# An input projection's four groups formed as seven quarter products instead of eight, in a hybrid stick-breaking and mLSTM block on Trainium2

## What is computed

```python
u = _rmsnorm(h, pre_norm_w[i])
proj = u @ w_in[i]                      # 2048 x 1024 by 1024 x 4616
sb_q, sb_k, sb_v, sb_z, ml_q, ml_k, ml_v, ml_o, ml_z, ml_i, ml_f = _split_cols(proj)
y_sb = _stick_breaking_attention(...)   # 8 heads of 64, causal
qk = silu(_causal_conv(concat([ml_q, ml_k]), ml_conv_w[i], ml_conv_b[i]))   # 4 taps over tokens
y_ml = _mlstm_chunkwise(...)            # 4 heads of 128
y = concat([y_sb, y_ml]) @ w_out[i]     # after norms and gates
h = h + _rmsnorm(y, post_norm_w[i])
h = h + sigmoid(h @ ple_w_gate[i] + ple_b_gate[i]) * (p[i] @ ple_w_up[i])
```

## Time and profile before

| what | us |
|---|---|
| runs | 1811.83, 1808.72, 1812.38; median 1811.83 |
| span of the profiled execution | 1808.6 |
| its own time beside the span | not recorded; the runs' median is 3.2 above the span, their least 0.1 |
| first stage, tiles / groups / gates on TensorE | 8.2 to 116 / 116 to 472 / 472 to 487 |
| TensorE busy | 1761.9, 97% |
| VectorE, ScalarE, GpSimd busy | 1119.1, 991.3, 680.6 |

### The profile page before, as it was taken

The page is one execution under the profiler, slowest core; times in us unless marked ns, Lnnn a source line. Parts: engine busy times, 40 slices in busy tenths (PEclk is TensorE's granted clock), DMA queues, the critical chain, the costliest instruction groups (busy, mean ns, idle before and its releaser), DMA issues. The chain is left out here.

```text
span 1808.6 us, 28177 instructions
## 1 busy us (share of the span) xinstructions
PE 1761.9 (97%) x8972; PEld 1437.3 (79%) x8972; DVE 1119.1 (62%) x1776; ACT 991.3 (55%) x2041; POOL 680.6 (38%) x942
## 2 busy tenths in 40 slices
PE   7999999999899999999999999998999999999998
PEld 6888888878577887888878887886788888788887
DVE  5431214555479898979797979894666666533333
ACT  5431213322277787878787878784677776411111
POOL 1100000000147777777777777772234444200000
PEclk9999999999999999999999999999999999999999
DMA  6677766121394647454656453735555454422220
GB/s 199 163 192 215 232 186 186 52 87 47 126 282 131 172 144 212 135 175 135 174 171 185 135 176 127 249 118 190 169 193 159 162 189 139 162 77 79 81 82 40
DMA packets 193733, 277.05 MB, mean 153 GB/s; under 512 B 66684, under 2 KB 128380, under 8 KB 184408
## 3 DMA queue, kind: packets, MB, share of 16 engines
q1 hardware_dynamic: 190952, 265.19, 47.8%
q0 software_dynamic: 2672, 10.52, 1.7%
HBM read 187.41 MB, written 88.26 MB: 152 GB/s over the span
## 5 line engine op out<-in xcount | busy, mean ns | idle before, releaser
L975 PE MATMUL b_late<-w_split,spare 128*128 128x512 f32 x1416 | 411.4, 415 | 2.5 <-ACT b_p_out L1057 2.3
L756 POOL TENSOR_TENSOR b_a_lo<-b_aT,b_a_hi 128x512 fp32r<-128x512 f32 (+2 forms) x312 | 354.8, 1137 | 25.0
L1138 DVE TENSOR_TENSOR_SCAN b_buf<-b_y,b_buf 128x511 f32<-128x511 f32 (+2 forms) x320 | 357.9, 1118 | 9.1
L529 PE MATMUL a_po<-uT_hi,w_split 128*128 128x512 f32 x1024 | 318.6, 392 | 2.3 <-DVE w_split L397 2.3
L975 PEld LDWEIGHTS b_late<-w_split,spare 128*128 128x128 f32 x1416 | 243.4, 190 | 40.5 <-issue 4.6
L752 POOL CAST b_a_hi<-b_aT 128x512 fp32r<-128x512 f32 (+1 forms) x320 | 182.1, 569 | 179.1 <-PE b_o L949 147.6
L1148 DVE SCALAR_TENSOR_TENSOR b_buf<-b_buf,b_y 128x512 f32<-128x512 f32 (+2 forms) x320 | 187.9, 587 | 70.0 <-PE b_y L935 69.0
L529 PEld LDWEIGHTS a_po<-uT_hi,w_split 128*128 128x128 f32 x1024 | 193.0, 188 | 46.4 <-DVE w_split L397 2.7
L1034 ACT ACTIVATE b_aT<-b_turned 128x512 f32<-128x512 f32 (+1 forms) x320 | 170.3, 532 | 67.6 <-POOL b_a_lo L756 60.1
L529 PE MATMUL a_po<-uT_lo,w_split 128*128 128x512 f32 x512 | 201.6, 394 | 0.0
L1043 ACT ACTIVATE b_buf<-b_y 128x512 f32<-128x512 f32 (+2 forms) x320 | 171.3, 535 | 50.1 <-PE b_y L929 47.7
(11 more groups left out here) (244 smaller groups left out, 3359.6 us busy)
## 6 DMA issues: line engine op xcount, KB each, us to landing
spare<-u_pair SPq DMA_DIRECT2D x62, 1024.0 KB, 5.4
proj_n<-b_p_out SPq DMA_DIRECT2D x59, 256.0 KB, 5.7
c_gates<-proj_n SPq DMA_DIRECT2D x16, 768.0 KB, 4.5
w_raw<-in_w_in POOLq DMA_DIRECT2D x5, 2048.0 KB, 10.1
x_in<-in_x SPq DMA_DIRECT2D x16, 512.0 KB, 3.9
qk_hi<-stage_hi SPq DMA_DIRECT2D x32, 256.0 KB, 2.6
qk_lo<-stage_lo SPq DMA_DIRECT2D x32, 256.0 KB, 2.9
u_pair<-uT_hi SPq DMA_DIRECT2D x16, 512.0 KB, 3.7
```

Source lines behind the costliest of these rows:

```text
L529: mm = pe.matmul(po[t][:], w[:, k, m * P:(m + 1) * P], u[:, k, t * GROUP:(t + 1) * GROUP], start=(k == 0 and n == 0), stop=(k == KT - 1 an ...
L756: nc.gpsimd.tensor_tensor(lo[:, cols], raw, hi[:, cols].bitcast(F32), ALU.subtract).then_inc(lo_done, 1)
L975: mm = pe.matmul(late[:], u_in[f % US][:, u_part, k, :], w[:, k, :], start=(i == 0), stop=(i == PASSES - 1))
L1138: nc.vector.tensor_tensor_scan(down, y[u % YS][:, 1:keys][:, ::-1], down, b[:, keys - 1:keys], ALU.add, ALU.subtract).then_inc(log_done, 1)
```

## The change

The 16 tiles are done in two blocks of eight. After the tiles of a block come its gate columns, and then its eight quads. A quad is 256 output columns by 1024 tokens of one of the groups 4, 5, 0, 1 (in this order, two quads a group; the first four of a block are convolved). In a quad, weights and activations are each cut in halves of depth and of columns or tokens, and the product of 2 by 2 quarters is formed as seven quarter products instead of eight (a Strassen-Winograd scheme). Each is 4 depth tiles by 3 parts, 12 matmuls of 128x128 by 128x512, whose moving side is four runs of 128 tokens.

- The four sums of activation quarters (t1 to t4) are formed once a block, during its tiles 4 to 7, t1 and t2 by VectorE, t3 and t4 by GpSimd, then split into hi and lo (`token_sums`, `high_t`, `low_t`).
- The four sums of weight quarters (s1 to s4) are formed by GpSimd in each quad, and GpSimd, not VectorE, makes the lo part of all seven weight operands (`low`). GpSimd's queue loads a quad's weights, 1 MB in rows of 1 KB, after the sixth lo part of the quad before (`load_pair`).
- The banks X, Y and Z take the products. ScalarE copies the first product out (`copy_p1`), VectorE forms the four outputs from it and the banks. The convolution's first tap and bias are a ScalarE activation that reads PSUM; VectorE adds the other three, also out of PSUM, and the few tokens across tile ends on their own (`halo_taps`).
- The loops over groups are written out. The late group's weights go to a place of their own and are split in the last four quads.
- In the second stage the first late tile's 24 matmuls are all at step 0 and before its score, the constants are waited for after it, and the clearing of semaphores follows the constants and the mLSTM's. The load of that tile's activations is now the last thing that the first stage issues, and that stage waits for all its stores to land.

The core of the diff, with TensorE's, ScalarE's, VectorE's and GpSimd's new order:

```diff
+PRODUCTS = (("a11", "b11", "x", True), ("s2", "t2", "y", True), ("a12", "b21", "x", False), ("s3", "t3", "y", False),
+            ("s1", "t1", "z", True), ("a22", "t4", "y", False), ("s4", "b22", "z", False))
@@ tensor
+            def product(q, s):
+                pe.wait_ge(op_lo_done, SLOTS * q + s + 1)
...
+                if s == 2:
+                    pe.wait_ge(p1_done, q + 1)
+                if s == 3:
+                    pe.wait_ge(u2_done, q + 1)
+                if s == 5:
+                    pe.wait_ge(u3_done, q + 1)
+                if s == 6:
+                    pe.wait_ge(c22_done, q + 1)
...
+                for k in range(HALF):
+                    for m, (w_part, u_part) in enumerate(PARTS):
+                        mm = pe.matmul(out, w_ops[:, s, w_part, k, :], u[home][:, :, u_part, k, :],
-            with pe.Fori(1, GROUPS) as g:
-                group(g)
+            turn(0)
+            for b in range(BLOCKS):
...
+                values(TILES * b + TILES - 1)
+                for h in range(2):
+                    gates(2 * b + h)
+                for q in range(PER * b, PER * (b + 1)):
+                    for s in range(SLOTS):
+                        if q == PER - 1 and s == SLOTS - 1:
+                            turn(TILES)
+                        product(q, s)
@@ scalar
+            def high(t):
+                for h in range(2):
...
+                    nc.scalar.copy(homes(t)[h][:, 0], turned).then_inc(u_hi_done, 1)
+                    if j < HALF:
...
+                        nc.scalar.copy(u_raw[j][h], turned).then_inc(u_raw_done, 1)
+            def quad(q):
+                copy_p1(q)
+                silu_before(2)
+                if not first:
+                    next_op(0)
+                silu_before(3)
+                if not first:
+                    next_op(1)
+                if conv:
+                    first_tap(q, 0)
+                else:
+                    high_c(q, 0)
+                if not first:
+                    next_op(2)
+                if q == PER - 1:
+                    square(TILES)
+                if not first:
+                    next_op(3)
+                if conv:
+                    first_tap(q, 1)
+                    silu(q, 0)
+                else:
+                    high_c(q, 1)
+                if first:
+                    for s in range(4):
+                        next_op(s)
+                next_op(4)
+                if conv:
+                    first_tap(q, 2)
+                    silu(q, 1)
...
+                next_op(5)
@@ vector
+            def convolve_quad(q):
+                sum_with_p1(q, 1, 1, u2_done)
+                taps(q, 0)
+                nc.vector.tensor_copy(c11_end, X[:, GROUP - HALO:]).then_inc(c11_end_done, 1)
+                first_halo(q, 0)
+                sum_with_p1(q, 3, 3, u3_done)
+                sum_with_z(q, 4, 3, po[0][:], u3_done, c22_done)
+                taps(q, 1)
...
+                nc.vector.tensor_tensor(Y[:], p1, Y[:], ALU.add).then_inc(c21_done, 1)
+                taps(q, 2)
@@ gpsimd, a block's tile step, first quad and later quads
+                    if j + 1 < TILES:
+                        reciprocal_root(TILES * b + j + 1)
+                    if 0 <= j - 5 < HALF:
+                        low_t3(b, j - 5)
+                    if 0 <= j - 4 < HALF:
+                        token_sums(b, j - 4)
+                        low_t2(b, j - 4)
+                low(q0, 0)
+                sum_s1(q0)
+                sum_s2(q0)
+                low(q0, 1)
+                low(q0, 2)
+                sum_s3(q0)
+                low(q0, 3)
+                low(q0, 4)
+                sum_s4(q0)
+                low(q0, 5)
+                load_pair(q0 + 1)
+                low(q0, 6)
+                for q in range(q0 + 1, q0 + PER):
+                    sum_s1(q)
+                    sum_s2(q)
+                    sum_s3(q)
+                    sum_s4(q)
+                    for s in range(SLOTS):
+                        low(q, s)
+                        if s == 5 and q + 1 < q0 + PER:
+                            load_pair(q + 1)
@@ second stage
+            if f == 0:
+                return f, range(PASSES if n == 0 else 0)
-            pe.wait_ge(consts_ready, 3)
             for n in range(STEPS):
...
+                if n < LATE_STEPS:
+                    project(n)
                 if n == 0:
                     score(n)
-                if n < LATE_STEPS:
-                    project(n)
+                    pe.wait_ge(consts_ready, 3)
```

More of the change, by code:

```diff
@@ L176, in input_projection, with taps_before, conv_tile @@
+        def taps_before(q, n):
+            return sum((CONV_K - 1) * (2 if has_halo(m, i) else 1) for m in range(q + 1) if is_conv(m)
+                       for i in CONV_ORDER[:4 if m < q else n])
+        def conv_tile(q, i):
+            return (QUADS[q][1] - 4) * TG + 2 * QUADS[q][2] + i // 2
         block = ctx.enter_context(nc.Block())
@@ new lines, in first_tap @@
+            def first_tap(q, n):
+                i, b = CONV_ORDER[n], q // PER
+                m = conv_tile(q, i)
+                if n == 0:
+                    if convs_before[q] == 0:
+                        act.wait_ge(conv_w_loaded, 16 * (CONV_K + 1))
+                    act.wait_ge(product_done, SLOTS * q + 3)
+                else:
+                    act.wait_ge({3: c22_done, 2: c21_done, 1: c12_done}[i], q + 1)
+                until(act, hi_stored[i], 16 * q)
+                if i < 2 and q % PER == 0:
+                    act.wait_ge(gates_stored[i], 16 * (b + 1))
+                nc.scalar.activation(stage[i][:].bitcast(F32), conv_source(i), ACT.Identity, bias=cb[:, m:m + 1],
+                                     scale=cw[:, m, CONV_K - 1:CONV_K]).then_inc(first_tap_done, 1)
@@ new lines, in sum_with_z, with low_c @@
+            def sum_with_z(q, s, i, out, before, done):
+                dve.wait_ge(before, q + 1)
+                dve.wait_ge(product_done, SLOTS * q + s + 1)
+                nc.vector.tensor_tensor(out, c_of(i), Z[:], ALU.add).then_inc(done, 1)
+            def low_c(q, n):
+                i, g = C_ORDER[n], QUADS[q][1]
+                dve.wait_ge(c_hi_done, 4 * pairs_before[q] + n + 1)
+                if n == 0:
+                    c_free(q, 0)
+                nc.vector.scalar_tensor_tensor(out=c_of(i), in0=X[:] if n == 0 else c_of(i),
+                                               scalar=-SB_SCALE if g == 1 else 1.0, in1=stage[i][:].bitcast(F32),
+                                               op0=ALU.mult, op1=ALU.subtract).then_inc(c_lo_done, 1)
@@ new lines, in taps @@
+            def taps(q, n):
+                i, m = CONV_ORDER[n], conv_tile(q, CONV_ORDER[n])
+                source, out = conv_source(i), stage[i][:].bitcast(F32)
+                dve.wait_ge(first_tap_done, 4 * convs_before[q] + n + 1)
+                for count, j in enumerate(range(CONV_K - 1)):
+                    late = CONV_K - 1 - j
+                    if count:
+                        dve.wait_ge(tap_done, taps_before(q, n) + count)
+                    nc.vector.scalar_tensor_tensor(out=out[:, late:], in0=source[:, 0:GROUP - late], scalar=cw[:, m, j:j + 1],
+                                                   in1=out[:, late:], op0=ALU.mult, op1=ALU.add).then_inc(tap_done, 1)
@@ new lines, in halo_taps @@
+            def halo_taps(q, n, before):
+                i, m = CONV_ORDER[n], conv_tile(q, CONV_ORDER[n])
+                out = stage[i][:].bitcast(F32)
+                for j in range(CONV_K - 1):
+                    late = CONV_K - 1 - j
+                    dve.wait_ge(tap_done, taps_before(q, n) + CONV_K - 1 + j)
+                    nc.vector.scalar_tensor_tensor(out=out[:, 0:late], in0=before[:, j:HALO], scalar=cw[:, m, j:j + 1],
+                                                   in1=out[:, 0:late], op0=ALU.mult, op1=ALU.add).then_inc(tap_done, 1)
@@ new lines, in gates @@
+            def gates(n):
+                b, h = n // 2, n % 2
+                free_values(TILES * (b + 1) + n)
+                if n == 0:
+                    pe.wait_ge(wg_lo_done, 1)
+                    pe.wait_ge(wg_hi_done, 2)
+                    pe.wait_ge(wg_zeroed, 1)
+                pe.wait_ge(u_lo_done, 2 * TILES * (b + 1))
+                out = po[(TILES * (b + 1) + n) % 3][0:2 * GATES, :].rearrange("p (s t) -> p s t", s=HALF)
+                for k in range(KT):
+                    home = ((u["b11"], u["b21"]), (b12, u["b22"]))[h][k // HALF]
+                    for m, (w, part) in enumerate(((wg_hi, 1), (wg_pair, 0))):
+                        mm = pe.matmul(out, w[:, k, :], home[:, :, part, k % HALF, :],
+                                       start=(k == 0 and m == 0), stop=(k == KT - 1 and m == 1))
+                mm.then_inc(gates_done, 1)
@@ L727, in _ @@
         def _(pool):
-            for s in ended:
-                pool.sem_clear(s)
```

945 lines of the change are left out of this document (601 added, 344 removed).

## The result

The changed kernel takes 1839.85 us (median of 4 runs, 1837.89 to 1843.59) against 1811.6: a ratio of 1.0156, 95% interval [1.014, 1.0172]. It is 28 us slower, where 14 us faster was forecast. Its profiled execution took 1841.2 us, with a span of 1839.4; the two profiled executions lie 30.8 us apart, the medians 28.

A forecast was written before the change was run, and what follows sets the result against it. TensorE was taken as the bound: 44.5 us saved by 192 fewer matmuls, less 1.1, 3.0, 4.8, 11.7, 7.6 and 2.2 of added waits, gives 14.1 less, 1797.7 us taken as 1798; range 1778 to 1820.

The forecast's parts named there:

- rival 3: Quad matmuls: a moving side in four runs costs more, 0.25 us per matmul; 1822 us, chance 0.05.
- The wait between the blocks: TensorE waits for tile 9's scaling and tile 8's lo part behind the last quad: 5.9 us.
- The start: First tile: its lo part waits for two raw copies beside two hi copies; 1.1 us, range 0 to 1.2.
- the first late tile's end: Where the stages meet: activations land at about 8.1 us, then 24 matmuls, to 16.0 after the last product.
- the convolved quads: Later convolved quads: product 5 waits for sum U3 behind the next weight load and ScalarE's queue; 11.7 us in all.
- half clock: TensorE's clock at 0.50 behind the wait between the blocks; 1.7 us more there.
- the first quads: First quad of each block: product 2 waits for ScalarE's copy of product 0; 2.4 us each, 4.8 for both.
- the issue of the next load: GpSimd's next weight load: issued 1.9 us into a convolved quad, 4.6 in a block's second, 0.5 in groups 0 and 1.
- Tiles 4 to 7: Tiles of each block: a ring of 8.75 us against TensorE's 6.49; 1.5 us a block, 3.0 for both, bounds 0 to 6.
- The seam: Where the first stage meets the next: 21.0 us against 18.8 before, 2.2 more; bounds -3 to +5.
- rival 2: Weight-load ring becomes the bound at product 5's wait for U3; landing 10 us gives 1833, decisive from 8.3; chance 0.09.
- Rival 1: Chains hold: convolved quads cost 4, tiles 1, stage seam 0; 29 us less, 1783; chance 0.28.

The follow-up runs named there:

- e13: Changed kernel with ScalarE's first tap of output 0 placed between the copies of the next quad's operands 0 and 1: 1820.85 us, ratio 1.0063.
- e4: Changed kernel with extra matmuls that nobody reads put into TensorE's queue where it stood idle: 1830.51 us, ratio 1.0104.
- e1: Changed kernel with ScalarE's first tap of output 0 ahead of the copies of the next quad's operands 0 and 1: 1817.63 us, ratio 1.0029.
- e8: Changed kernel with a quad's weights loaded in two halves of 512 KB, after GpSimd's fourth and sixth lo parts: 1827.13 us, ratio 1.0083.
- e6: Changed kernel with ScalarE's copy of product 0 ahead of s4's hi part in a block's first quad: 1835.68 us, ratio 1.0131.
- e7: Changed kernel with the first late tile's activations loaded before the last quad's stores, second queries right behind the first: 1839.7 us, ratio 1.0146.

## Why the prediction was wrong

**What held.** The 192 matmuls are saved in full, and rival 3 is refuted the other way: those with four runs of 128 stand 0.2267 us apart (12 in 2.72). The 0.2316 of the earlier trace rows is an average that holds the loop's gaps; without them it was 0.229, and why the rest is shorter now no run shows. With the tiles that was 8.9 us in its favour, which it had not foreseen. The wait between the blocks is right (5.9 against 5.5). The start came out at 1.1 partly by luck: 0.64 is the wait for the raw copies, 0.43 a first turn that was later anyway. So did the first late tile's end, 16.0 us after the last product, forecast and measured: the activations landed 0.7 us later than forecast (8.8 against 8.1), and the 24 matmuls took 7.2 us where 7.9 were put. The mechanism of the convolved quads is right too: product 5 waits for U3, that for the taps, those for the first tap behind the copy behind the sums behind the load. The rows of quad 1 show these links, and e13 takes two of them out. From landing to product 5 it took 7.2 us in quad 1; 6.85 was forecast.

**The step that failed first: the clock, charged at one place.** In the first stage the forecast priced half clock only behind the 6 us between the blocks, 1.7 us, from the earlier trace rows. It put it at nothing behind the waits that it forecast itself, of 2.4 us in the first quads and 3.5 and 4.0 in quads 1 and 9, and gave no reason. Between the first tile and the last product there were sixteen waits of 1.1 us and more. Waits of 3.9 to 7.1 us were followed by 1.9 to 3.3 us of lost rate (quads 0, 1, 8, 9), those of 2.3 us in quads 3 and 11 by 2.0 and 2.2, while others of 1.6 to 2.2 us cost 0.3 more. e4 shows half clock as a cost of its own. In size the miss is 23.8 us if all that is left in the table is put to it, and about 17 by the 19 us that go with the clock.

**The second, as large: the issue of the next load.** The forecast followed ScalarE's chain to operand 5 and put the issue at 1.9 into a convolved quad, 4.6 into a block's second and 0.5 into one of groups 0 and 1. It did not follow GpSimd's own queue. Four sums and six lo parts stand there between a landing and the next issue: in quads 5 and 6 the first sum is at 208.93 and the next issue at 222.77, 13.8 us, which with 7.4 for the landing is a period of 21.3 against TensorE's 19.04. "GpSimd has 11, 13.9 us of 19.5" counted them as covered, but an engine that waits for its own load has only the quad less the landing. GpSimd in quads 5 and 6 (line 262 is the issue, 284 the first of the four sums):

```profile
201.51 0.90 POOL L262 DMA_DIRECT2D w_raw<-in_w_in  x1 [0.30 <-POOL w_ops L300]
...
208.93 1.30 POOL L284 TENSOR_TENSOR w_raw<-w_raw 128x512 f32<-128x512 f32 x1 [5.20 <-DMA w_raw<-in_w_in]
...
214.02 8.45 POOL L300 TENSOR_TENSOR w_ops<-w_raw,w_ops 128x512 fp32r<-128x512 f32 x6
222.77 0.90 POOL L262 DMA_DIRECT2D w_raw<-in_w_in  x1 [0.30 <-POOL w_ops L300]
```

Measured, the issue stood at 6.5 into quad 1 (112.39 - 105.90) and 3.0 into quad 5 (201.51 - 198.49), and the landing, 6.0 forecast, was 7.6 and 7.4 there. It was 6.2 for the loads issued in quads 2 to 4, with the DMA engines as busy (0.66 of the time, against 0.63 and 0.65), so what made those two later is not shown. 1.9 and 1.6 us more in quad 1 made its larger wait; 2.5 and 1.4 in quads 5, 6, 13, 14 turned "2 to 3 us to spare" into waits of 1.7 to 2.0. That is 17.5 us over the ten quads (29.2 of waits where 11.7 were forecast). The damage came from both: a queue on which the late load stood ahead of the work that TensorE waited for (e1 takes this out, with loads still 20.3 us apart, and the waits go), and a ring longer than TensorE's period (e8 shortens it and leaves the queue, and half of the gain of e1 comes).

**The others.** Tiles 4 to 7: the ring is 10.1 and 10.4 us instead of 8.75 (the t2 sums follow each other at 37.64, 47.78 and 58.17), mainly because VectorE's scale took 2.23 instead of the 1.28 of the earlier trace rows while GpSimd worked. The first quads took 4 us more; e6, where their waits fall to 1.5 and 1.4, shows that ScalarE's order was in them, but gives 1.7 and 2.0 back in the next quad. The seam: the first late tile ended where it was forecast, but the second load of queries, issued behind the first late activations, held score 4 for 4 us; e7 removes that and the time does not move, so how much of the seam's 5.4 us is the order and how much the clock stays open.

The Trainium skill (SBUF — State Buffer, SBUF: two separate sides) says that the pair of ports which VectorE and GpSimd share goes to one of them for a whole instruction, and the other stands still, where VectorE reads both inputs from SBUF. The trace agrees that the two slow each other: the split of an output of groups 0 and 1, both inputs in SBUF, took mostly 1.2 to 1.6 us beside GpSimd's lo parts, and 0.69 in a block's last quad, when GpSimd had none left; GpSimd's lo parts took 1.45 on average in those quads against 1.29 in the convolved ones. The prediction named it as a way into rival 2; it is a part of the ring there. Six lo parts, 1.42 us from start to start instead of 1.24, make it 1.1 us longer.

Rival 2 came nearest, and its place was right, but the point that it gave, a landing of 8.3 us, was not reached (7.6 at most), nor were the matmuls further apart: neither sign that it named for being wrong came. The kernel was slower by more than it said with landings that it called harmless. Rival 1's sum is 3 us off by its own terms (44.5 - 1.1 - 1 - 4.8 - 4 - 7.6 is 26.0, not 29), which changes nothing here.

## What to carry to other kernels

When one engine waits for its own load, its period is the landing plus all of its work, and that sum is compared with the other engine's period, not the busy time alone. On an in-order queue, work that waits for a far thing (a load, another engine's sums) goes behind the work that the busiest engine will ask for next; this single exchange of places was worth 22 us, and once it was right the shorter load gained nothing that these runs can tell. A new idle stretch on TensorE can have a second price at half clock, here 0.3 to 3.3 us, and is to be charged with it wherever it stands; and when one link of a wait is taken out, look at once at which link is only just shorter.

## What the runs showed of the hardware

- Half clock is not proportional to the wait before it: 2.3 us of wait cost 2.0 more in quad 3, 2.2 us cost 0.3 in quad 10. In seven profiled executions with the same seam the stretch from it to the third stage differed by up to 6.4 us.
- Matmuls of 128x128 by 128x512 in fp32r stand 0.2267 us apart with the moving side in four runs of 128 tokens. Those of group 2 in the same kernel, with one run of 512, stand 0.2267 apart too (12 in 2.72, 67.32 to 70.04), so the four runs cost nothing. In the kernel before it was 0.229 with one run (129.68 to 148.45 in its loop).
- A load issued by GpSimd kept it busy for 0.90 us (1 MB) and 0.77 us (512 KB) at the issue, and landed after 6.2 and 4.3 us (medians). The Trainium skill (DMA: Bandwidth & Descriptors, Bandwidth) gives 6.15 for 1 MB, of the transfer alone and without the writing of its descriptors. The 6.2 measured is from issue to landing, so it is near that figure but not the same quantity.
